# A hybrid attention and RWKV-7 layer on one core: the RWKV preparation laid out anew over the slots of the loop

## The chip, the cores and the metric

One core of a Trainium2 chip runs the whole program. The metric is device microseconds of one execution. The kernel before takes 1856.16 us (median of 3 runs, 1854.52 to 1862.93).

## The reference, cut to what matters

One layer over 1024 frames of width 1024: a projection, then attention with low-rank keys and values (8 heads) beside an RWKV-7 group (8 heads of 64), an output projection, cross-attention to 256 memory tokens, an MLP with squared ReLU, and norms between. The change lies in the RWKV group and its neighbours:

```
w_log = -softplus(-(w0 + tanh(w_l) @ w2)) - 0.5      # low-rank product "lw"
decay = exp(-exp(w_log))
a     = sigmoid(a0 + a_l @ a2)                        # low-rank product "la"
kk    = heads(k * k_k); kk /= max(norm(kk), 1e-12)    # sums of squares "ks"
k     = k * (1 + (a - 1) * k_a)
# per head and frame:
sa    = state @ (-kk_t)
state = state * decay_t + outer(sa, kk_t*a_t) + outer(v_t, k_t);  y_t = state @ r_t
y     = groupnorm(y) + sum(r * k * r_k) * v           # sums "rk", products "bv" (the bonus)
```

The recurrence is computed by chunks of 64 frames. Each chunk needs the inverse of a unit lower triangular 64x64 matrix built from products of keys ("al"). All is float32.

## The kernel before, in words

**Engines and order.** Each engine runs one list of instructions in the order in which it was written; waits are on counters (`Steps`) that name every step. Heads are taken in pairs, so the RWKV group has 4 pairs. Between 0 and about 390 us the core normalises, projects, and runs attention heads 0 to 5. Heads 6 and 7 follow, with the preparation of RWKV pair 0 beside them; then the RWKV loop over pairs 0 to 3, with the preparation of the next pair beside each (the memory tokens beside the last). From about 812 us on come the memory projections, the output projection, cross-attention and the MLP.

**The loop.** A pair has 8 windows of 128 frames, taken two at a time: 4 groups of 11 slots, 44 slots. In a group, TensorE does `double_q` and `double_z` twice (two levels that grow the inverse from blocks of 16 to 64; VectorE masks the first and adds the second), which are followed by slots 0, 1, 2, 3; then `solve`, `local`, `carry`, followed by slots 4, 5, 6; then four steps of `state`, `outputs`, and the next group's `scores` and `tokens`, followed by slots 7 to 10. VectorE's order around slots 4 to 6 is: slots 4 and 5, then the transition matrix (`mt`, line 2582: the carry product from PSUM plus a diagonal that GpSimd made), then slot 6, then per state one copy (line 2592) and for two of them the masked scores (line 2447). TensorE's first `state` of a group waits for `mt`.

**The preparation `prep(n, s)`** exists on TensorE, ScalarE, VectorE and GpSimd; slot s of one engine stands beside slot s of the others, and beside which work slot s comes is set by `beside` in the loop and by `beside_heads` in heads 6 and 7, which gives each of 18 places (9 a head) its slots. Its steps: TensorE lw0, lw1, la0, la1 (low-rank products, all in PSUM bank 7, so each waits for ScalarE's tanh of the one before), ks0, ks1 (sums of squares, each waits for a logarithm or square on ScalarE), al0 to al3 (16 products of 64x64 each, VectorE masks each), rk0, rk1 (bonus sums). VectorE kk, t1p, L (a scan), na, am, k2, nkk, kt, at, b, bt, rk, the masks of al, x0 and x1 (clearing the block table), bv0, bv1 and the substitution. ScalarE the tanh, square, logarithm and exponentials (W is the decay, Wi its inverse). GpSimd rt (needs W) and, after rk, kh and bh.

**The inverse.** The al matrices go from SBUF to DRAM in four stores (SyncE queue, `blocks`), come back as blocks of 16 by one load, and VectorE solves all blocks together: 15 steps j, each a product and a sum (`xm`, `xa`, lines 2412 and 2415), then a transposed copy (`xt`, 2418). Block and transpose are stored, and eight loads bring them back as chunks (`inverse`); the first doubling of a pair waits for four of them.

**Places.** `rAL` and `rXX` (al and inverse, two buffers each) lie in the attention's tiles: the outputs', queries', keys' and probabilities'. Pair 0's inverse lies over the probabilities. The last pair's slots hold the memory tokens' work: squares on ScalarE (slots 2, 3), sums on TensorE (slot 6), logarithm and exponential (slots 7, 8).

Of the kernel before, what the change touches and what calls it, by code (L numbers as in the profile page):

```python
# [12 lines left out]
ALU = mybir.AluOpType  # L13
# [14 lines left out]
SUBST = (range(0, 8), range(8, BLK - 1))  # L28
# [42 lines left out]
V_TILES = (0, 2, 3, 4, 7, 1, 5, 6)  # L71
# [93 lines left out]
def build(nc, x_t, mem_t, pos, wall, vecs, con_d, headw, wv_d, lora_d, out_t):  # L165
    with ExitStack() as ctx:
# [71 lines left out]
        def place(n):  # L238
# [232 lines left out]
        def each(names):  # L471
# [4 lines left out]
        P_ACT = Steps(sem("prep_act"), each(["tw0", "tw1", "ta0", "ta1", "kksq", "kl0", "kl1", "kf", "W", "Wi", "wt0", "wt1", "afirst"]))  # L476
        P_DVE = Steps(sem("prep_dve"), each(
            ["kk", "t1p", "L", "na", "am", "k2", "nkk", "kt", "at", "b", "bt", "rk",
             "al0", "al1", "al2", "al3", "x0", "x1", "bv0", "bv1"]
            + [x for j in range(BLK - 1) for x in (f"xm{j}", f"xa{j}")] + ["xt"]))  # L480
# [73 lines left out]
        def _(sp):  # L554
# [76 lines left out]
            def inverse(n):  # L631
# [9 lines left out]
                if n == 0:  # L641
                    sp.wait_ge(M_PE.sem, M_PE.at(f"o{MLA_HEADS - 1}_{NW - 1}", -1))
# [262 lines left out]
        def _(pe):  # L905
# [239 lines left out]
            def prep(n, s):  # L1145
# [14 lines left out]
                if s == 3:  # L1160
                    r_at(P_ACT, f"tw0_{n}")
                    low_rank(lora_wa[wa, 0:P], wa, T_CQWA, 7, 1).then_inc(sem_, one("lw1"))
                if s == 4:
                    r_at(P_ACT, f"tw1_{n}")
                    low_rank(lora_wa[wa, P:2 * P], wa, T_CQWA, 7, 0).then_inc(sem_, one("la0"))
                if s == 5:
                    r_at(P_ACT, f"ta0_{n}")
                    low_rank(lora_wa[wa, P:2 * P], wa, T_CQWA, 7, 1).then_inc(sem_, one("la1"))
# [214 lines left out]
            def beside(p, s):  # L1383
# [6 lines left out]
                elif s == 6:  # L1390
# [260 lines left out]
        def _(act):  # L1651
# [104 lines left out]
            def prep(n, s):  # L1756
# [5 lines left out]

                if s in (2, 3):
                    if s == 2 and n >= 1:
                        r_at(P_DVE, f"rk_{n - 1}")
                    r_at(P_PE, f"lw{s - 2}_{n}")
                    nc.scalar.activation(rT1[:, halves(s - 2)], PS[:, 7, :], ACT.Tanh, bias=vech[:, n:n + 1],
                                         scale=0.5).then_inc(sem_, one(f"tw{s - 2}"))
                if s in (4, 5):
                    r_at(P_PE, f"la{s - 4}_{n}")  # L1770
                    nc.scalar.activation(rA[:, halves(s - 4)], PS[:, 7, :], ACT.Tanh, bias=vech[:, 4 + n:5 + n],
                                         scale=0.5).then_inc(sem_, one(f"ta{s - 4}"))
# [10 lines left out]
                if s == 10:  # L1783
                    r_at(P_ACT, f"kl1_{n}")
                    nc.scalar.activation(rB[i], rB[i], ACT.Exp, scale=-0.5).then_inc(sem_, one("kf"))
# [4 lines left out]
                    nc.scalar.activation(rW, rWi, ACT.Exp, scale=-half_e).then_inc(sem_, one("W"))  # L1790
                if s == 11:
# [75 lines left out]
            def memory_step(s):  # L1867
# [3 lines left out]
                if s in (2, 3):  # L1871
                    act.wait_ge(mem_loaded, 32)
                    nc.scalar.activation(mem_sq[s - 2], mem_raw[s - 2], ACT.Square).then_inc(mm_act, 1)
                if s == 7:
# [3 lines left out]
                if s == 8:  # L1878
# [263 lines left out]
        def _(dve):  # L2142
# [182 lines left out]
            def prep(n, s):  # L2325
# [14 lines left out]
                if s == 4:  # L2340
                    r_at(P_ACT, f"tw1_{n}")
                    r(nc.vector.tensor_scalar(rT1, rT1, 1.0, None, ALU.add), "t1p")
                if s == 5:
# [4 lines left out]
                if s == 9:  # L2348
                    r_at(P_ACT, f"ta1_{n}")
                    r(nc.vector.tensor_scalar(rA, rA, -0.5, -0.5, ALU.mult, ALU.add), "na")  # L2350
                if s == 10:
                    own("na")
                    r(nc.vector.tensor_scalar(rT1, rA, 1.0, vec[:, V_KA + n:V_KA + n + 1], ALU.add, ALU.mult), "am")
                if s == 14:
# [19 lines left out]
                if s == 20:  # L2374
                    own("b")
                    r(nc.vector.tensor_tensor(rB[i], rA, rWi, ALU.mult), "bt")
                if s == 21:
                    r_at(P_POOL, f"rt_{n}")
                    r(nc.vector.scalar_tensor_tensor(r_, r_, vec[:, V_RK + n:V_RK + n + 1], rT1, ALU.mult, ALU.mult), "rk")
                if 22 <= s < 26:  # L2380
                    k = s - 22
# [9 lines left out]
                if s == 26:  # L2391
# [5 lines left out]
                if s in (26, 27):  # L2397
                    k = s - 26
# [4 lines left out]
                if 30 <= s < 37:  # L2403
                    for j in range(2 * (s - 30), 2 * (s - 30) + 2 + s // 36):
# [11 lines left out]
                if s == 36:  # L2416
# [562 lines left out]
```

## Time and profile before

| | |
|---|---|
| median of 3 runs | 1856.16 us |
| profiled execution, its own time | 1852.6 us |
| its span (first to last instruction) | 1850.5 us |
| TensorE busy | 1741.0 us, 94% |
| VectorE busy | 992.4 us, 54% |
| ScalarE busy | 793.5 us, 43% |
| GpSimd busy | 703.9 us, 38% |
| mean granted TensorE clock | 0.970 |

In rows, PE is TensorE (PEld its weight loads), DVE VectorE, ACT ScalarE, POOL GpSimd, SPq the SyncE queue; L12 is line 12 of the kernel; [...] is the idle time before an instruction and what ended it. A timeline row is start, duration (us), engine, line, operation, output<-input, count. A row of a window is its ends and length, then the busy time (and instructions) of PE, PEld, DVE, ACT and POOL, the granted clock, the share of the DMA engines and GB/s.

The granted clock is a share of 2.4 GHz: 1.00 is that level, 0.50 is 1.2 GHz. Matmuls are pipelined, so the durations of neighbours overlap. The chain that ended last is TensorE for 84% of the span and VectorE for 8%. Heads 6 and 7 take about 390 to 480 us, the four pairs of the loop about 484 to 812 us.

### The profile page before, as it was taken

To read this page: it belongs to the slowest core of one execution; us is meant where nothing else is said; L and a number is where in the kernel's file an instruction comes from. 1 tells how busy PE (TensorE), PEld (TensorE's weight loads), DVE (VectorE), ACT (ScalarE), POOL (GpSimd) and SP (SyncE) were. 2 spreads that over 40 slices of the span, in tenths; PEclk is the share of its full clock that TensorE was granted. 3 is DMA by queue.
4 is the path that set the end of the run, shared out by engine and by line. 5 is a ranking of instruction groups with operands and counts; after the bars stand their busy time and mean duration, and the time that the engine had idled before them with its cause. 6 is when DMAs were issued, how large, how long until landed. Compare 5 with 4: busy or idle time off the path is not lost.

```text
span 1850.5 us, 29970 instructions
## 1 busy us (share of the span) xinstructions
PE 1741.0 (94%) x11908; PEld 1332.4 (72%) x11908; DVE 992.4 (54%) x1549; ACT 793.5 (43%) x1530; POOL 703.9 (38%) x505
## 2 busy tenths in 40 slices
PE   4999999998788889899999999999999999999996
PEld 3766666655566666668898768778888888888885
DVE  6542232335464655463350262378856775884787
ACT  4313332244233343452130231367566666766762
POOL 1220211011120211232242202297695876968761
PEclk9999999988689999999999999999999999999998
DMA  5101010001111112242211101212112022020202
GB/s 195 53 24 32 23 34 10 21 5 29 41 19 42 20 43 42 88 145 87 88 41 51 34 1 34 76 50 69 50 42 92 23 69 67 26 92 23 69 1 91
DMA packets 81681, 94.35 MB, mean 51 GB/s; under 512 B 53648, under 2 KB 56208, under 8 KB 81552
## 3 DMA queue, kind: packets, MB, share of 16 engines
q1 hardware_dynamic: 81552, 92.56, 15.9%
q8 instruction: 89, 1.46, 0.3%
q14 instruction: 40, 0.33, 0.1%
HBM read 82.57 MB, written 9.98 MB: 50 GB/s over the span
## 4 chain that ended last, share of the span: by engine, by line
PE 84%; DVE 8%; issue 3%; ACT 2%; DMA 1%; POOL 1%; SPq 0%; DVEq 0%; ACTq 0%; POOLq 0%
PE PS L1615 32%; PE PS L922 16%; PE PS L970 8%; PE PS L1071 3%; PE PS L1106 2%; PE PS L1085 2%; PE PS L1140 2%; PE PS L1562 1%; PE PS L1541 1%; PE PS L1433 1%; PE PS L1143 1%; PE PS L1335 1%; PE PS L1418 1%; PE PS L1277 1%; PE PS L1030 1%
## 5 line engine op out<-in xcount | busy, mean ns | idle before, releaser
L1615 PE MATMUL PS<-memr,wsp 128*128 128x512 f32 x1332 | 321.2, 392 | 0.9 <-POOL wsp L883 0.9
L922 PE MATMUL PS<-xn,wsp 128*128 128x512 f32 x1344 | 309.6, 392 | 6.7 <-DVE xn L2158 6.7
L922 PEld LDWEIGHTS PS<-xn,wsp 128*128 128x128 f32 x1344 | 253.5, 189 | 62.0 <-DVE xn L2158 5.0
L1615 PEld LDWEIGHTS PS<-memr,wsp 128*128 128x128 f32 x1332 | 250.6, 188 | 56.0 <-POOL wsp L883 1.3
L762 POOL CAST wsp<-wraw 128x1024 fp32r<-128x1024 f32 x40 | 43.4, 1085 | 472.9 <-PE PS L922 306.5
L1615 PE MATMUL PS<-memr,wraw_r 128*128 128x512 f32 x684 | 167.7, 394 | 5.4 <-DVE memr L2721 3.3
L1615 PEld LDWEIGHTS PS<-memr,wraw_r 128*128 128x128 f32 x684 | 129.0, 189 | 35.2 <-DVE memr L2721 3.7
L970 PE MATMUL PS<-xn,wsp 128*128 128x512 f32 x576 | 146.7, 401 | 3.2 <-DVE proj L2208 3.1
L883 POOL TENSOR_TENSOR wsp<-sa,wsp 128x512 fp32r<-128x512 f32 x86 | 115.1, 1340 | 81.0 <-ACT wsp L2047 80.9
L970 PEld LDWEIGHTS PS<-xn,wsp 128*128 128x128 f32 x576 | 104.4, 188 | 40.1 <-issue 20.2
L2721 DVE TENSOR_TENSOR memr<-PS,memr 128x512 fp32r<-128x512 f32 x168 | 114.6, 682 | 27.4 <-ACT PS L2068 27.4
L1727 ACT ACTIVATE H<-PS,mst 128x128 f32<-128x128 f32 (+3 forms) x64 | 47.5, 741 | 179.8 <-DVE mst L2289 178.2
L1615 PE MATMUL PS<-tmp_r,wsp 128*128 128x512 f32 x444 | 116.9, 397 | 0.0
L2739 DVE TENSOR_TENSOR H<-PS,H 128x512 f32<-128x512 f32 x128 | 86.7, 688 | 46.7 <-PE PS L1615 30.1
L2289 DVE TENSOR_REDUCE mst<-PS 128x1 f32<-128x128 f32 (+3 forms) x64 | 48.2, 754 | 117.3 <-PE PS L1074 117.3
L2063 ACT CAST memr<-sa 128x512 fp32r<-128x512 f32 x96 | 59.2, 617 | 95.1 <-PE PS L1615 78.6
L1615 PEld LDWEIGHTS PS<-tmp_r,wsp 128*128 128x128 f32 x444 | 83.4, 188 | 21.2 <-DVE tmp_r L2721 1.3
L764 POOL TENSOR_TENSOR wsp<-wraw,wsp 128x1024 fp32r<-128x1024 f32 x40 | 96.4, 2410 | 3.2
L867 POOL TENSOR_TENSOR sbx<-sa,sbx 128x512 f32<-128x512 f32 x64 | 85.9, 1342 | 4.7
L883 POOL TENSOR_TENSOR wsp<-sbx,wsp 128x512 fp32r<-128x512 f32 x62 | 82.9, 1341 | 11.1 <-ACT wsp L2047 11.0
L847 POOL TENSOR_TENSOR ssum<-con,rsm 64x256 f32<-64x256 f32 x32 | 27.3, 871 | 139.5 <-DVE ssum L2582 139.5
L1071 PE MATMUL PS<-H 128*128 128x512 f32 (+2 forms) x192 | 77.2, 512 | 0.0
(336 smaller groups left out, 3157.4 us busy)
## 6 DMA issues: line engine op xcount, KB each, us to landing
wraw<-in_weights_dram SPq DMA_DIRECT2D x40, 512.0 KB, 3.6
sa<-in_weights_dram SPq DMA_DIRECT2D x32, 512.0 KB, 4.3
H<-in_x_dram SPq DMA_DIRECT2D x16, 512.0 KB, 6.5
sbx<-in_weights_dram SPq DMA_DIRECT2D x32, 256.0 KB, 2.6
sa<-in_weights_dram SPq DMA_DIRECT2D x32, 256.0 KB, 2.6
H<-in_weights_dram SPq DMA_DIRECT2D x8, 512.0 KB, 6.7
out_dram<-sbx SPq DMA_DIRECT2D x16, 256.0 KB, 2.1
a_dram<-H SPq DMA_DIRECT2D x16, 128.0 KB, 2.5
```

Source lines behind the costliest of these rows:

```text
L764: nc.gpsimd.tensor_tensor(wsp[:, k, :, 1, :], raw, wsp[:, k, :, 0, :].bitcast(F32), ALU.subtract).then_inc(w_split, 1)
L867: nc.gpsimd.tensor_tensor(out, a, b, op).then_inc(W_SUM.sem, W_SUM.one(name))
L883: nc.gpsimd.tensor_tensor(w[:, 1, :], w_source(g), w[:, 0, :].bitcast(F32), ALU.subtract).then_inc(mw_rest, 1)
L922: last = nc.tensor.matmul(PS[:, 2 * k + half, :], wsp[:, k, kt, a, :], src[:, at, b, HALF * half:HALF * half + HALF], start=(i == 0 and (a ...
L970: last = nc.tensor.matmul(PS[:, bank, :], wsp[:, u % 2, kt, a, :], xn[:, kt, b, HALF * half:HALF * half + HALF], start=(kt == 0 and (a, b) ...
L1071: nc.tensor.matmul(PS[:, b + part, 0:n], mQ[:, win(q)], mK[:, HALF * part:HALF * part + n], start=True, stop=(part < q // 4))
L1615: last = nc.tensor.matmul(PS[:, g % PS_BANKS, :], w[:, a, win(k)], x[:, b, :], start=(k == 0 and (a, b) == (0, 0)), stop=(k == ROWS - 1 an ...
L1727: nc.scalar.activation(mP[q % 2][:, 0:n], two(2 * (q % 2))[:, 0:n], ACT.Exp, bias=mNeg[hd][:, q:q + 1], accum_out=mSum[h // 2 % 2][:, c:c ...
L2063: nc.scalar.copy(x_split_of(d)[:, 0, :], x_source(d)).then_inc(mx_head, 1)
L2289: m(nc.vector.tensor_reduce(mNeg[h % 2][:, q:q + 1], two(2 * (q % 2))[:, 0:P * (q + 1)], AX_X, ALU.max, negate=True), f"m{h}_{q}")
L2721: nc.vector.tensor_tensor(x[:, 1, :], PS[:, PS_BANKS + d % 2, :], x[:, 0, :].bitcast(F32), ALU.subtract).then_inc(mx_rest, 1)
L2739: out(nc.vector.tensor_tensor(tile, a, b, ALU.add), f"{kind}{part}_{v}")
```

## The change

Slots are laid out anew, and places with them; no instruction is added or taken away.

- TensorE and ScalarE: the four low-rank products and their tanh go from slots 2 to 5 to slots 0 to 3; al0 to al3 from 22-25 to 18-21; rk0 and rk1 from 26, 27 to 31, 32.
- VectorE: t1p and L to slot 3 (beside kk), na and am to 4, k2 from 14 to 5, bt from 20 to 16, the masks of al to 18-21 and rk behind them in 21, x0 and x1 from 26 to 24, bv0 and bv1 to 31 and 32.
- Substitution: steps 0 to 14 in slots 30 to 36 before; after, 0-3 in 26, 4-7 in 27, 8 in 29, 9 in 30, 10 and 11 in 31, 12 and 13 in 32, 14 (and the transposed copy) in 33.
- ScalarE in slot 10: W ahead of kf.
- Places: the first inverse (`rXX[0]`) lies over queries and keys, `rAL[1]` over probabilities; the loads of the first inverse wait for the last scores instead of the last attention values. `V_TILES`, the order in which tiles of H take memory weights and x, follows.
- Last pair: squares in slots 5 and 6, sums in slot 9, logarithm and exponential in 10 and 11.

```diff
-SUBST = (range(0, 8), range(8, BLK - 1))
+SUBST = {26: (0, 1, 2, 3), 27: (4, 5, 6, 7), 29: (8,), 30: (9,), 31: (10, 11), 32: (12, 13), 33: (14,)}
+BONUS = 31
-V_TILES = (0, 2, 3, 4, 7, 1, 5, 6)
+V_TILES = (0, 1, 2, 4, 7, 3, 5, 6)
...
-        rAL = [hs_[:, S * n:S * n + S].rearrange("p (w h n) -> p w h n", w=NW, h=2) for n in range(2)]
-        rXX = [hs_[:, 3072 + 2048 * n:5120 + 2048 * n].rearrange("p (a w h n) -> p a w h n", a=2, w=NW, h=2)
-               for n in range(2)]
+        rAL = [hs_[:, t:t + S].rearrange("p (w h n) -> p w h n", w=NW, h=2) for t in (0, 3072)]
+        rXX = [hs_[:, t:t + 2048].rearrange("p (a w h n) -> p a w h n", a=2, w=NW, h=2) for t in (1024, 5120)]
...
             i = 9 * (h - BESIDE) + q
-            if i < 8:
-                return (2 * i + 1, 2 * i + 2) if h >= BESIDE else ()
-            return ((17, 20), (21,), (22, 23), (24, 25), (26, 27), (), (30, 31), (32, 33), (34, 35), (36,))[i - 8]
+            if h < BESIDE:
+                return ()
+            if i < 9:
+                return (2 * i, 2 * i + 1)
+            return ((), (18, 19), (20, 21, 22), (24,), (), (26, 27), (29, 30, 31), (32, 33), ())[i - 9]
...
                 if n == 0:
-                    sp.wait_ge(M_PE.sem, M_PE.at(f"o{MLA_HEADS - 1}_{NW - 1}", -1))
+                    sp.wait_ge(M_PE.sem, M_PE.at(f"s{MLA_HEADS - 1}_{NW - 1}", -1))
...                                                                         # TensorE
-                if s == 2:
+                if s == 0:
                     pe.wait_ge(lora_loaded, 16 * (n + 1))
...                                                                         # lw1, la0, la1: slots 1, 2, 3
-                if 22 <= s < 26:
-                    k = s - 22
+                if 18 <= s < 22:
+                    k = s - 18
                     if k == 0:
                         r_at(P_ACT, f"kl1_{n}")
-                        r_at(P_DVE, f"rk_{n}")
+                        r_at(P_DVE, f"bt_{n}")
...
-                if s == 26:
-                    r_at(P_DVE, f"al3_{n}")
+                if s == BONUS:
+                    r_at(P_DVE, f"rk_{n}")
                     block_sums(0, C_BO, proj[:, T_R + n, :], 7).then_inc(sem_, one("rk0"))
-                if s == 27:
+                if s == BONUS + 1:
...                                                                         # ScalarE
                 if s == 10:
-                    r_at(P_ACT, f"kl1_{n}")
-                    nc.scalar.activation(rB[i], rB[i], ACT.Exp, scale=-0.5).then_inc(sem_, one("kf"))
                     r_at(P_DVE, f"L_{n}")
...
                     nc.scalar.activation(rW, rWi, ACT.Exp, scale=-half_e).then_inc(sem_, one("W"))
+                    r_at(P_ACT, f"kl1_{n}")
+                    nc.scalar.activation(rB[i], rB[i], ACT.Exp, scale=-0.5).then_inc(sem_, one("kf"))
...
-                if s in (2, 3):
+                if s in (5, 6):
                     act.wait_ge(mem_loaded, 32)
...                                                                         # VectorE: the slots listed above
-                if 30 <= s < 37:
-                    for j in range(2 * (s - 30), 2 * (s - 30) + 2 + s // 36):
+                if s in SUBST:
+                    for j in SUBST[s]:
```

## Rows read from the trace of the kernel before

**Rows 1.** page, busy time of TensorE: us, share, instructions.
```profile
PE 1741.0 (94%) x11908; PEld 1332.4 (72%) x11908; DVE 992.4 (54%) x1549; ACT 793.5 (43%) x1530; POOL 703.9 (38%) x505
```

**Rows 2.** PE's waits, 480 to 812 us (total us, times, longest).
```profile
PE PS L1366 <- DVE ssum L2582: 11.1, 6, 3.1
```

**Rows 3.** timeline of pair 1, group 1 (start, us, engine, line).
```profile
603.11 2.35 POOL L792 TENSOR_TENSOR sa<-proj,sa 128x1024 f32<-128x1024 f32 x1 [30.47 <-ACT sa L1790]
...
604.06 2.48 DVE L2356 SCALAR_TENSOR_TENSOR sa<-sa,proj 128x1024 f32<-128x1024 f32 x1
...
611.82 0.68 DVE L2582 TENSOR_TENSOR ssum<-PS,ssum 128x512 f32<-128x512 f32 x1
...
612.55 0.45 PE L1366 MATMUL PS<-tmp,ssum 128*64 128x64 f32 x4 [3.10 <-DVE ssum L2582]
```

**Rows 4.** windows: doubling in groups 0 to 3, then three state chains.
```profile
578.20:584.11 5.91, 5.44 (x84) 3.31 (x84) 3.14 (x9) 0.69 (x1) 0.00 (x0) 1.00 0.58 159
600.05:603.83 3.78, 3.50 (x87) 2.78 (x83) 2.25 (x7) 3.77 (x6) 0.72 (x1) 1.00 0.02 4
619.70:624.38 4.68, 4.61 (x153) 4.37 (x151) 3.46 (x11) 1.22 (x2) 3.51 (x2) 1.00 0.11 25
639.88:644.93 5.05, 3.24 (x86) 2.69 (x83) 4.30 (x21) 2.34 (x4) 0.00 (x0) 1.00 0.00 0
612.55:619.70 7.15, 6.50 (x87) 5.13 (x88) 4.48 (x8) 2.08 (x9) 1.49 (x3) 0.76 0.01 2
632.67:639.88 7.21, 6.30 (x94) 4.43 (x94) 4.23 (x18) 3.54 (x11) 1.07 (x2) 1.00 0.01 2
653.55:659.50 5.95, 5.04 (x87) 3.90 (x88) 2.38 (x6) 2.02 (x9) 1.07 (x2) 1.00 0.74 168
```

**Rows 5.** groups of VectorE instructions by line: busy us, mean ns of one.
```profile
L2415 DVE TENSOR_TENSOR sc_s<-sc_s 128x15 f32<-128x15 f32 (+7 forms) x60 | 12.5, 208 | 2.1
...
L2347 DVE TENSOR_TENSOR_SCAN sa<-step,sa 128x1024 f32<-128x1024 f32 x4 | 9.2, 2289 | 0.1
...
L2402 DVE TENSOR_TENSOR proj<-PS,proj 128x512 f32<-128x512 f32 x8 | 5.5, 692 | 14.8 <-PE PS L1143 14.7
...
L2353 DVE TENSOR_SCALAR sa<-sa,vec 128x1024 f32<-128x1024 f32 x4 | 3.0, 740 | 0.0
```

**Rows 6.** timeline of head 6: the same k2 with GpSimd idle.
```profile
423.49 1.21 DVE L2356 SCALAR_TENSOR_TENSOR sa<-sa,proj 128x1024 f32<-128x1024 f32 x1
```

**Rows 7.** timeline, then DMA issues (last: us to landing), pair 1.
```profile
624.58 0.42 DVE L2387 TENSOR_TENSOR H<-PS,con 128x256 f32<-128x256 f32 x1 [0.39 <-PE PS L1187]
...
628.17 0.37 SPq L629 DMA_DIRECT2D sc_s<-a_dram  x1
...
sc_s<-a_dram SPq DMA_DIRECT2D x1, 128.0 KB, 3.2
```

**Rows 8.** stretches at the lower clock: busy by engine, granted clock.
```profile
477.80:511.40 33.60, 29.41 (x268) 20.62 (x266) 8.35 (x19) 8.23 (x18) 4.37 (x3) 0.50 0.20 49
532.40:540.00 7.60, 6.93 (x74) 5.48 (x76) 4.63 (x10) 1.27 (x6) 1.18 (x2) 0.56 0.01 2
...
644.90:648.30 3.40, 3.37 (x44) 3.15 (x44) 3.16 (x10) 0.74 (x2) 0.00 (x0) 0.50 0.23 28
...
750.80:754.00 3.20, 3.20 (x67) 2.85 (x65) 0.00 (x0) 1.66 (x2) 0.00 (x0) 0.50 0.36 141
```

**Rows 9.** timeline of the last pair, group 0.
```profile
746.25 1.06 ACT L1873 ACTIVATE sa<-sa 128x1024 f32<-128x1024 f32 x1 [2.44 <-DMA sa<-in_mem_dram]
...
748.56 0.34 PE L1323 MATMUL PS<-sc_w,sc_s 64*64 64x64 f32 x8 [2.23 <-ACT sc_s L1951]
```

**Rows 10.** timeline of head 7: bonus sum, transposes of block 6.
```profile
453.05 1.13 PE L1143 MATMUL PS<-proj,con 128*128 128x512 f32 x2 [1.63 <-DVE proj L2402]
...
466.61 0.96 PE L1085 MATMUL PS<-con,H 128*128 128x128 f32 x7 [1.68 <-ACT H L1736]
```

**Rows 11.** chain of waits ahead of the loop: start, us, what.
```profile
474.87 4.07 DMA xt_dram<-sc_s
```

More of the change, by code:

```diff
@@ L475, in build @@
                                            "rk0", "rk1"]))
-        P_ACT = Steps(sem("prep_act"), each(["tw0", "tw1", "ta0", "ta1", "kksq", "kl0", "kl1", "kf", "W", "Wi", "wt0", "wt1", "afirst"]))
+        P_ACT = Steps(sem("prep_act"), each(["tw0", "tw1", "ta0", "ta1", "kksq", "kl0", "kl1", "W", "kf", "Wi", "wt0", "wt1", "afirst"]))
         P_DVE = Steps(sem("prep_dve"), each(
-            ["kk", "t1p", "L", "na", "am", "k2", "nkk", "kt", "at", "b", "bt", "rk",
-             "al0", "al1", "al2", "al3", "x0", "x1", "bv0", "bv1"]
-            + [x for j in range(BLK - 1) for x in (f"xm{j}", f"xa{j}")] + ["xt"]))
+            ["kk", "t1p", "L", "na", "am", "k2", "nkk", "kt", "at", "b", "bt", "al0", "al1", "al2", "al3", "rk", "x0", "x1"]
+            + [x for place in SUBST for x in ([f"bv{place - BONUS}"] if place in (BONUS, BONUS + 1) else [])
+               + [y for j in SUBST[place] for y in (f"xm{j}", f"xa{j}")]] + ["xt"]))
         P_POOL = Steps(sem("prep_pool"), each(["rt", "kh", "bh"]))
@@ L1159, in prep @@
                     low_rank(lora_wa[wa, 0:P], wa, T_CQWA, 7, 0).then_inc(sem_, one("lw0"))
-                if s == 3:
+                if s == 1:
                     r_at(P_ACT, f"tw0_{n}")
                     low_rank(lora_wa[wa, 0:P], wa, T_CQWA, 7, 1).then_inc(sem_, one("lw1"))
-                if s == 4:
+                if s == 2:
                     r_at(P_ACT, f"tw1_{n}")
                     low_rank(lora_wa[wa, P:2 * P], wa, T_CQWA, 7, 0).then_inc(sem_, one("la0"))
-                if s == 5:
+                if s == 3:
                     r_at(P_ACT, f"ta0_{n}")
@@ L1389, in beside @@
                     prep(p + 1, s)
-                elif s == 6:
+                elif s == 9:
                     memory_sums()
@@ L1761, in one @@
                     return P_ACT.one(f"{name}_{n}")
-                if s in (2, 3):
[L1764 to L1772, printed above, removed]
+                if s in (0, 1):
+                    if s == 0 and n >= 1:
+                        r_at(P_DVE, f"rk_{n - 1}")
+                    r_at(P_PE, f"lw{s}_{n}")
+                    nc.scalar.activation(rT1[:, halves(s)], PS[:, 7, :], ACT.Tanh, bias=vech[:, n:n + 1],
+                                         scale=0.5).then_inc(sem_, one(f"tw{s}"))
+                if s in (2, 3):
+                    r_at(P_PE, f"la{s - 2}_{n}")
+                    nc.scalar.activation(rA[:, halves(s - 2)], PS[:, 7, :], ACT.Tanh, bias=vech[:, 4 + n:5 + n],
+                                         scale=0.5).then_inc(sem_, one(f"ta{s - 2}"))
                 if s == 5:
@@ L1877, in memory_step @@
                                          scale=1.0 / D).then_inc(mm_act, 1)
-                if s == 8:
+                if s == 11:
                     act.wait_ge(mm_act, 3)
@@ L2347, in prep @@
                     r(nc.vector.tensor_tensor_scan(rWi, rStep, rT1, 0.0, ALU.mult, ALU.add), "L")
-                if s == 9:
+                if s == 4:
                     r_at(P_ACT, f"ta1_{n}")
                     r(nc.vector.tensor_scalar(rA, rA, -0.5, -0.5, ALU.mult, ALU.add), "na")
-                if s == 10:
+                if s == 4:
                     own("na")
                     r(nc.vector.tensor_scalar(rT1, rA, 1.0, vec[:, V_KA + n:V_KA + n + 1], ALU.add, ALU.mult), "am")
-                if s == 14:
+                if s == 5:
                     own("am")
@@ L2373, in prep @@
                     r(nc.vector.tensor_tensor(rA, rA, rKK, ALU.mult), "b")
-                if s == 20:
+                if s == 16:
                     own("b")
                     r(nc.vector.tensor_tensor(rB[i], rA, rWi, ALU.mult), "bt")
[L2377 to L2381, printed above, removed]
+                if 18 <= s < 22:
+                    k = s - 18
                     r_at(P_PE, f"al{k}_{n}")
@@ L2390, in prep @@
                         f"al{k}")
-                if s == 26:
+                if s == 21:
+                    r_at(P_POOL, f"rt_{n}")
+                    r(nc.vector.scalar_tensor_tensor(r_, r_, vec[:, V_RK + n:V_RK + n + 1], rT1, ALU.mult, ALU.mult), "rk")
+                if s == 24:
                     if n >= 1:
@@ L2396, in prep @@
                     r(nc.vector.memset(sc_s[:, 3456:3712:BLK + 1], 1.0), "x1")
-                if s in (26, 27):
-                    k = s - 26
+                if s in (BONUS, BONUS + 1):
+                    k = s - BONUS
                     r_at(P_PE, f"rk{k}_{n}")
```

10 lines of the change are left out of this document (5 added, 5 removed).

## The prediction

> **What bounds the kernel.** I read the page first, then the rows of who waited for whom on TensorE, then the timeline of one pair of the RWKV loop, then busy time and granted clock by stretch, and last the chain of waits ahead of the loop. TensorE (PE) is busy 94% of the span [rows 1], and everything outside 390 to 812 us is untouched but for places of buffers. So the question is what PE loses inside that stretch. It holds heads 6 and 7 of the attention (to about 480 us, with the first pair's preparation beside them) and four pairs of about 82 us, each of four groups. A group is: doubling (a ping-pong of small products and VectorE masks, slots 0 to 3), solve, local and carry (slots 4 to 6), then the chain of four states (slots 7 to 10). The next pair's preparation is cut into 44 slots over these groups, in program order on every engine, so a long VectorE step in a slot holds whatever the loop wants of VectorE behind it.
>
> The largest such loss is PE waiting for the transition matrix (the sum that reads the carry product): 11.1 us in 6 waits [rows 2]. The timeline of group 1 shows why: VectorE begins five preparation steps at 604.06 (k2, nkk, kt, at, b), reaches the matrix at 611.82, and PE starts again at 612.55, 3.1 us late [rows 3]. Three pairs have this wait. The rest is spread: doubling in group 3, where substitution sits in slots 0 to 3, takes 5.05 us against 3.78 in a group with nothing beside it [rows 4], and waits are followed by stretches at the lower clock level.
>
> **The change, part by part.** Terms are per pair unless said; gains are negative.
>
> *Low-rank products two slots sooner (pairs 1 and 2, group 0).* Doubling with two of them takes 5.91 us, without any 3.78 [rows 4]: 1.06 each, none of it hidden. Two move from the solve part into doubling: the same PE time. VectorE then has all of kk, t1p, the scan, na, am and k2 before the matrix: 2.29 for the scan [rows 5], four simple ones of at most 0.74 [rows 5], k2 at 1.21 as it runs when GpSimd leaves it alone [rows 6]: 6.4 us. PE needs 5.6 us from the end of doubling (603.83 [rows 4]) to its wait (612.55 less 3.10 [rows 3]) and has a key sum of 1.06 in slot 6 to fill the rest. So the matrix is just about not late, and the wait that the key sum had for the squared keys goes. I take -0.5, between +1.0 (it is late and nothing fills) and -1.0.
>
> *k2 out of group 1, bt into it, W ahead of kf.* Five steps before, five after: k2 (2.48 us [rows 3]) gives way to bt, which has the shape of k2 alone (1.21). k2 was long because it started while GpSimd's rt ran (603.11 for 2.35) [rows 3]: 605.46 plus 1.2 is its end. With W first, rt starts some 1.05 us sooner and overlaps the first step by some 0.35 instead of 1.27. So 7.76 becomes 6.85: -0.9, and a wait of 2.2 remains. Bounds: -2.1 if rt is out of the way wholly, 0 if nkk inherits the whole delay. The Trainium skill, "SBUF — State Buffer", section "Who interferes with whom", says that an instruction of VectorE with two inputs in SBUF and one of GpSimd that reads SBUF exclude each other, whoever came first, with no sharing. By that rule moving bt in front of the matrix costs its full turn behind any diagonal product, and the term would be nearer 0; the row on k2 agrees with it.
>
> *Score products of the inverse (al) from slots 22-25 to 18-21.* Beside doubling the four cost 4.68 less 3.78, 0.9 in all [rows 4]: -0.9 there. In the state chain of group 1 they come instead of bt and rk alone. That chain takes 7.15 us (at a mean clock of 0.76), a bare one 5.95 [rows 4]. I take +1.2, between 0 (the chain's own gaps take them) and +3.5 (they are paid in full at the lower level).
>
> *Substitution and bonus sums in group 2.* The two bonus sums have the shape of a low-rank product: -2.1 from the solve part. There VectorE now does 16 substitution instructions of 0.21 [rows 5], with their gaps 0.235: 3.75 us inside PE's 5.6. But they need the blocks read back. Before, the last mask begins at 624.58, the read is issued at 628.17 and lands 3.2 us later [rows 7]: 6.8 from mask to landing. The mask will lie about 0.8 ahead of doubling, VectorE is free for slot 4 some 4.0 after doubling begins (604.06 less 600.05 [rows 3, 4]), so it waits about 2.0 and ends 5.7 after that point: 0.1 to 0.2 over. Net -1.9. In the state chain of group 2 (7.21 with one sum of the post step and 12 substitution instructions [rows 4]) come two bonus sums, 2.1, and their two VectorE products of 0.69 [rows 5], one of them in front of a state copy: +2.6, between +1.5 and +4.
>
> *Group 3's doubling freed.* 5.05 becomes 3.8 to 3.9 (the last step and the transpose stay in slot 0): -1.2. The stretch at half clock right behind it, 644.9 to 648.3 with PE busy 3.37 of 3.40 [rows 8], and its like one pair later (two in all) should not arise: -1.7 each. The inverse ends three slots sooner, in front of loads that are hidden in most pairs: nothing counted.
>
> *Last pair.* ScalarE squares the memory tokens in slots 2 and 3, waits there for the load, and so copies the solved product late: PE idles 2.23 us [rows 9] and 3.2 us at half clock follow with PE busy throughout [rows 8]: 1.6. Behind both copies, in slots 5 and 6, the load (there at 746.25 [rows 9]) has landed: -3.5 with a little left. The memory sums move into the state chain at the same PE cost: 0.
>
> *Heads 6 and 7.* The second bonus sum no longer waits 1.63 for the first [rows 10], and both sums (2.1) go where PE waits for row maxima (1.68 at 466.61 [rows 10]); against that, eight more substitution instructions sit before the maximum of block 6 (+2.0, partly the same wait), and in head 6 lw1 waits for its tanh (0.8) while the key sums, now in one place, wait for one logarithm (1.7) instead of one square (1.7). I get -1.6 at the loop's start; bounds +3 and -5. The first pair's inverse may now be loaded once the last scores have read queries and keys. Its loads waited for the transpose's store (474.87 plus 4.07 [rows 11]), not for the attention's end, so this alone is 0; what counts is that the substitution ends about 2.3 sooner, which is in the -1.6.
>
> *First group of the loop.* 477.8 to 511.4 is at 1.2 GHz, PE busy 29.4 of 33.6 [rows 8]. Full clock would give back up to half of that. With four dense low-rank products inside doubling instead of two the rise may come sooner; the trace can't say. I take -2 of bounds +2 and -8.
>
> **Sum.** Group 0 twice -0.5: -1.0. Three times (-0.9 +1.2 -0.9 -1.9 +2.6 -1.2): -3.3. Clock behind group 3: -3.4. Last pair -3.5. Heads -1.6. First group -2.0. Together -14.8. The profiled execution took 1852.6 us (span 1850.5), so 1837.8; the median of the runs shown is 3.6 above it, so 1841.4. What lies behind the loop is PE-bound and moves with it.
>
> **Rivals.**
> A, the loss moves instead of going (28%). The state chain is serial between PE and VectorE; if al masks, bonus products and sums are paid in full there (+3.5 and +4 for +1.2 and +2.6: 11.1 more in three pairs), only -3.7 is left: 1852. For it: four states in 5.95 us leave 1.5 a step, and a sum of 1.06 with a product of 0.69 does not fit beside one. Against: the 12 substitution instructions and one sum added only 1.26 to it [rows 4].
> B, slower (12%): the block read is late. VectorE waits for it in slot 4 of group 2 in front of the matrix, PE idles behind. Up to about 6.8 us from mask to landing it costs nothing; each us more is one us in three pairs, and the idle of 3.1 us in group 1 was followed by up to 7.6 us at half clock (3.8 lost) [rows 8]. With store and read stretched from 3.6 and 3.2 to 5.7 each, 4.6 too late: 3 x (4.6 + 3.8) = 25 over the forecast, 1866.6. The threshold is the place where the sum has no slack at all; against it, the landing is the same transfer in the same company as before.
> C, the clock (inside my 60%): if the first group rises early and group 1 no longer drops, another 10 off: 1831.
>
> **How the numbers follow.** Forecast 60% (C in its lower part), A 28%, B 12%. A change of 0.5% (9.3 us) is about what a measurement of this kernel tells from none, so faster means below 1846.9 and slower above 1865.4. Nearly all of the forecast case is faster with a little of A; the forecast's upper tail joins A in same; B splits: faster 0.60, same 0.33, slower 0.07. Range 1831 to 1857: it holds the forecast case and A, and leaves out most of B and the far end of C.
>
> **What would show it.** Right: PE's wait for the matrix in group 1 is near 2.2, none over 1 in group 0; doubling of group 2 and 3 near 3.8; the state chain of group 2 near 9.8; no wait for a square in the last pair; substitution 0 to 7 starts about 2 us after VectorE is free. Wrong: group 2's matrix late by more than 1 us, new half-clock stretches behind the longer chains, or heads 6 and 7 longer than before.

## The result, and the profile after

| | before | after |
|---|---|---|
| median (runs) | 1856.16 us (11) | 1839.88 us (11) |
| profiled span | 1850.5 us | 1835.3 us |
| start of the loop | 484.13 us | 479.03 us |
| first `state` of the loop's last group | 808.66 us | 792.01 us |

The ratio is 0.9904, 95% interval 0.9887 to 0.9921. The forecast was 1841.4. The same kernel run once more, in a later series (x_again below), gave 1837.54 (6 runs).

Three names are used for the parts of a group: *doubling* runs from the first `double_q` product to the first `solve` product, the *solve part* from there to the first `state`, the *chain* from the first `state` to the next group's doubling.

First the busy times of the page. TensorE's hardly moved against [rows 1]: work was not taken away, waiting was.

```profile
PE 1737.6 (95%) x11908; PEld 1332.5 (73%) x11908; DVE 991.6 (54%) x1549; ACT 791.8 (43%) x1528; POOL 705.0 (38%) x505
```

PE's wait for the matrix over the whole span (total us, times, longest) is 9.2 us, to be laid beside [rows 2]; the longest is 2.3 instead of 3.1.

```profile
PE PS L1368 <- DVE ssum L2584: 9.2, 7, 2.3
```

The timeline of pair 1, group 1, to be laid beside [rows 3]. GpSimd's rt now starts 1.9 us ahead of VectorE's first step (nkk), not 0.95; nkk, kt and at take 1.55 to 1.63 beside GpSimd's instructions (at took 1.19 before, with GpSimd idle), b and bt 1.2. The five steps last 6.96 us up to the matrix instead of 7.76, and PE starts its first `state` 2.29 us late.

```profile
592.47 2.37 POOL L794 TENSOR_TENSOR sa<-proj,sa 128x1024 f32<-128x1024 f32 x1 [27.94 <-ACT sa L1790]
594.80 3.14 POOL L849 TENSOR_TENSOR ssum<-con,rsm 64x256 f32<-64x256 f32 x2
...
594.36 1.55 DVE L2361 SCALAR_TENSOR_TENSOR sa<-sa 128x1024 f32<-128x1024 f32 x1
595.84 1.63 DVE L2365 TENSOR_TENSOR proj<-sa 128x1024 f32<-128x1024 f32 x1
597.39 1.61 DVE L2370 TENSOR_TENSOR sa<-sa 128x1008 f32<-128x1008 f32 x1
598.93 1.21 DVE L2375 TENSOR_TENSOR sa<-sa 128x1024 f32<-128x1024 f32 x1
600.17 1.22 DVE L2378 TENSOR_TENSOR sa<-sa 128x1024 f32<-128x1024 f32 x1
601.32 0.68 DVE L2584 TENSOR_TENSOR ssum<-PS,ssum 128x512 f32<-128x512 f32 x1
...
602.06 0.45 PE L1368 MATMUL PS<-tmp,ssum 128*64 128x64 f32 x4 [2.29 <-DVE ssum L2584]
```

Windows after: a stretch at the lower clock behind that wait; the chain of group 2 of pair 1; and the chain of group 1 of pair 2. They answer to the chains of [rows 4] and the stretches of [rows 8]. Behind the same wait the clock fell in pairs 0 and 1 (about 14 us each, 525 to 539 and 603.5 to 617.5) and not in pair 2; before, it fell behind group 1 in all three pairs, for some 7, 4 and 7 us. Of the stretches behind group 3 (644.9 to 648.3 before, and its like) none is left.

```profile
603.00:618.00 15.00, 14.65 (x212) 12.88 (x206) 6.98 (x19) 3.44 (x11) 4.08 (x3) 0.54 0.21 41
...
624.71:632.53 7.82, 7.60 (x97) 4.64 (x97) 4.63 (x16) 3.71 (x11) 0.91 (x2) 1.00 0.01 2
683.10:690.06 6.96, 6.96 (x151) 6.15 (x152) 3.51 (x11) 2.15 (x9) 1.18 (x2) 1.00 0.20 44
```

**Where the 15.2 us of the span came from**, from the starts of the groups in the two timelines, beside the terms of the forecast:

| stretch | forecast | measured |
|---|---|---|
| up to the start of the loop (heads 6 and 7) | -1.6 | -5.1 (-1.05 of it ahead of head 6, in code that is the same) |
| pair 0, group 0 | -2.0 | -3.8 |
| group 0 of pairs 1 and 2 | -1.0 | -1.3 |
| group 1 of three pairs | +0.9 | +2.1 |
| group 2 of three pairs | -0.6 | -1.1 |
| group 3 of three pairs, with the clock behind it | -7.0 | -5.5 |
| last pair, up to the first `state` of its last group | -3.5 | -2.0 |
| behind that | 0 | +1.5 |
| together | -14.8 | -15.2 |

The +1.5 behind the loop goes with an early start: that part takes 1043.2 to 1043.3 us in the three kernels whose loop starts at 478 to 479 us (after, x_again, x_bonus) and 1040.2 to 1042.2 in all others.

### The profile page after: what moved, and what is told of

It reads as the page before. It is cut to its first block, busy times and chain, and to the rows that moved or that the text cites. A ratio compares the mean times of both kernels' runs of the same rounds, so it can differ in the third digit from the quotient of the medians.

```text
span 1835.3 us, 29968 instructions
## 1 busy us (share of the span) xinstructions
PE 1737.6 (95%) x11908; PEld 1332.5 (73%) x11908; DVE 991.6 (54%) x1549; ACT 791.8 (43%) x1528; POOL 705.0 (38%) x505
## 4 chain that ended last, share of the span: by engine, by line
PE 85%; DVE 8%; issue 2%; ACT 2%; POOL 1%; DMA 1%; SPq 0%; DVEq 0%; ACTq 0%; POOLq 0%
PE PS L1617 32%; PE PS L924 16%; PE PS L972 8%; PE PS L1073 3%; PE PS L1108 2%; PE PS L1087 2%; PE PS L1142 2%; PE PS L1564 2%; PE PS L1543 1%; PE PS L1435 1%; PE PS L1337 1%; PE PS L1420 1%; PE PS L1145 1%; PE PS L1032 1%; PE PS L1279 1%
## 5 line engine op out<-in xcount | busy, mean ns | idle before, releaser
L885 POOL TENSOR_TENSOR wsp<-sbx,wsp 128x512 fp32r<-128x512 f32 x62 | 83.1, 1344 | 10.9 <-ACT wsp L2049 10.8
```

What stands on the lines that cost most here:

```text
L885: nc.gpsimd.tensor_tensor(w[:, 1, :], w_source(g), w[:, 0, :].bitcast(F32), ALU.subtract).then_inc(mw_rest, 1)
```

## Experiments

All were timed against the kernel before, whose median was 1856.8 to 1861.4 in those series; ratios are to that median. "Loop" is the time from the first doubling of pair 0 to the first `state` of the last group: 324.5 us before, 313.0 after. "Starts" is when it begins: 484.1 and 479.0. Times of parts are from the profiled execution. In the edits ... marks lines that are left out.

**x_mem: the kernel before with only the memory tokens' work moved.**

```
-                elif s == 6:                    +                elif s == 9:
-                if s in (2, 3):  # squares      +                if s in (5, 6):
...                                                              # logarithm, exponential: slots 10, 11
```

> The kernel before with one edit: the memory tokens' squares in slots 5 and 6 of the last pair instead of 2 and 3, their sums in 9, logarithm and exponential in 10 and 11. Theory S (the gain is the sum of the slots' terms): the last pair's group 0 loses its 2.2 us wait and the stretch at half clock behind it, -2.8 to -3.5 us, about 1853. Rival (the load is late wherever it is waited for, or the memory sums stretch the state chain by as much): no difference, 1856.

1852.69 us (12 runs), ratio 0.9978 (0.9959 to 0.9998). Group 0 of the last pair takes 19.44 us instead of 22.47, at full clock throughout:

```profile
744.61:764.05 19.44, 17.72 (x320) 14.28 (x318) 7.56 (x17) 7.81 (x18) 4.51 (x4) 1.00 0.53 194
```

So 3 us of the forecast's 3.5 are there, by themselves. Here and in the whole change 0.8 of it is paid back in the next group (17.02 and 17.01 instead of 16.20).

**x_lr: the kernel before with only the low-rank products two slots sooner**, and what follows from them on VectorE up to k2, with W ahead of kf. Substitution, bt, al, bonus and memory stay.

> The kernel before with the low-rank products in slots 0 to 3, t1p and the scan in 3, na and am in 4, k2 in 5, and W ahead of kf; bt, al, bonus sums and substitution where they were. Theory S: group 1 has four VectorE steps before the matrix, its wait falls from 3.1 to about 1.0 us, group 0 changes by less than 1: -6 us by waits alone, down to -10 if the half-clock stretches behind group 1 go too: 1846 to 1850. Rival (the wait moves to group 0, where VectorE has 6.4 us before the matrix): at least 1 us of wait there in each pair and no more than -3 in all, 1853 or more.

1848.95 us (12 runs), ratio 0.9941 (0.9917 to 0.9965). The loop takes 314.6 us though the last pair's group 0 grew to 27.13 (ScalarE reaches the squares sooner, waits 5.20 us for the load, and holds the copies of the solved product; PE idles 4.98 us, and some 10 us at the lower clock follow). The wait of group 1 is 1.03 us, shorter than in the kernel after:

```profile
612.43 0.45 PE L1368 MATMUL PS<-tmp,ssum 128*64 128x64 f32 x4 [1.03 <-DVE ssum L2584]
```

Group 1 takes 16.45 us in pairs 0 and 1 (20.45 and 19.65 before), and in pair 2 17.64. The kernel after then puts bt (1.22 us) into this place: 1.03 plus 1.22 is 2.25 of its 2.29. The loop starts 7.6 us later than in the kernel before, which took most of the gain.

Here bt and rk are in the chain of group 1, as before, and where the clock stays up it takes 6.01 us, next to a bare one's 5.95 [rows 4]. In pair 2 the clock fell for 4 us behind the same wait of 1.03, and the chain takes 7.20.

```profile
612.43:618.44 6.01, 5.16 (x86) 4.02 (x88) 4.31 (x8) 2.03 (x9) 1.48 (x3) 1.00 0.01 3
```

Pairs 0 to 2 together take 242.7 us of this loop and 247.7 of the kernel after's. So in these profiles the steps that the kernel after moves besides (bt, al, bonus sums, substitution) cost more than they brought, as long as the wait of 2.29 us stays in; x_bonus and x_subst below show that the last two pay, which leaves bt and al. An estimate for this kernel with x_mem's edit, from the last pair's group 0 at 19.44 us instead of 27.13 and 0.8 paid back in the next: a loop of some 308 us, 5 below the kernel after. It was not run.

**x_late: the kernel after with the blocks read twice**, the second read in front of the substitution: rival B made true.

```
-                sp.dma_start(bA, blocks_in_dram(0)).then_inc(a_blocks_loaded, 16)
+                for k in range(2):
+                    sp.dma_start(bA, blocks_in_dram(0)).then_inc(a_blocks_loaded, 16)
+                    sp.wait_ge(a_blocks_loaded, 16 * (2 * n + k + 1))
...                                                              # VectorE waits for 32 * (n + 1)
```

> The kernel after, with the blocks of the inverse read twice in a row, so that substitution's input is there about 3.7 us later. Theory S with the mechanism of rival B: the matrix of group 2 comes 3 to 4 us later in each of three pairs, and half-clock stretches may follow: 1850 to 1860, against 1840 for the kernel after. Other theory (substitution has slack, since pairs 0 and 1 run at half clock there): at most +4, 1844 or less.

1851.22 us (12 runs), ratio 0.9965 (0.9943 to 0.9988): 11.3 above the kernel after, and the loop 12.9 longer. In pair 1 VectorE waits 5.62 us for the blocks and PE 3.56 for the matrix (2.29 in pair 0, 2.72 in pair 2), with 3.5 to 7 us at half clock behind each:

```profile
631.30 0.69 PE L1370 MATMUL PS<-tmp,ssum 128*64 128x64 f32 x4 [3.56 <-DVE ssum L2586]
...
631.30:641.45 10.15, 10.15 (x92) 6.05 (x94) 4.63 (x16) 3.18 (x10) 1.18 (x2) 0.70 0.01 2
```

The mechanism of B is real. In the kernel after the read lands in time: the same wait of VectorE is 1.13 us in pair 1 and 1.87 in pair 2, and PE reaches its first `state` after 6.50 us in both. In pair 1 VectorE still waits 0.38 us for the carry product before the matrix; in pair 2 the matrix stands directly behind the substitution, so there the slack is used up and nothing is lost.

**x_fill: the kernel after with PE kept busy in the wait of group 1.** Four 128x512 products whose result nothing reads go into slot 17. VectorE's work, and the time of the matrix, stay as they are.

```
+                if s == 17 and n >= 1:
+                    r_at(P_ACT, f"kl1_{n}")
+                    for _ in range(2):
+                        block_sums(0, C_BO, proj[:, T_GK, :], 7)
```

> The kernel after, with four extra matmuls of 128x512 (2.1 us, result unused) in slot 17 of pairs 0 to 2, where PE otherwise waits 2.29 us for the matrix of group 1. Theory I (it is this idle time that the clock answers to): no half-clock stretch begins behind group 1 in pairs 0 and 1, and their state chains fall from 10.2 to about 7 us, doubling of group 2 from 5.9 to 4.7: -8 to -9 us, about 1832. Theory W (it is the many small products around it, or chance of phase): the stretches stay and the time is 1840 or up to 1 us more.

1831.25 us (5 runs), ratio 0.9854 (0.9822 to 0.9887). Doubling, solve and matrix take what they took (solve to first state 7.92), but the idle is 0.38 instead of 2.29, and the chain behind is 6.97 in all three pairs:

```profile
602.21 1.98 PE L1145 MATMUL PS<-proj,con 128*128 128x512 f32 x4
...
604.83 0.45 PE L1372 MATMUL PS<-tmp,ssum 128*64 128x64 f32 x4 [0.38 <-DVE ssum L2588]
...
604.83:611.80 6.97, 6.97 (x151) 6.16 (x153) 3.51 (x11) 2.16 (x9) 1.18 (x2) 1.00 0.19 41
```

Adding work took 8.6 us off the median (6.3 against the later median of the kernel after), and 8.3 off the loop. VectorE's list up to the matrix is as long as it was, and the matrix comes at the same point, so it is PE's idle that costs: the chain that took 10.2 us in pairs 0 and 1 is the same instructions at the lower clock.

**x_warm: x_fill with 20 more such products around the first pair's scores**, to raise the clock for group 0 of pair 0.

```
...                                                              # warm(count): count pairs of 128x512 products
+                warm({scores: 2, tokens: 0, a_v: 8}[stage])
```

> The kernel with fillers in group 1's wait (1831), and ten extra matmul pairs of 128x512 around the first pair's scores: 2 pairs behind the scores, 8 behind the products a_v, where PE otherwise waits about 3 us for the inverse; results unused. Theory I: the clock is back at 2.4 GHz before or soon after the first doubling, and the first group takes 21 to 26 us instead of 33: less some 4 us of extra work, -3 to -8, 1823 to 1828. Rival (the half-clock stretch lasts as long whatever PE does): +6 to +14, since the fillers run at half clock and end behind the arrival of the inverse.

1831.69 us (5 runs), ratio 0.9855 (0.9835 to 0.9875). Group 0 of pair 0 falls from 33.3 us in x_fill to 27.44, and the loop starts at 489.82 instead of 485.66. The clock is up for the first 7 us of the loop and then half for 7 us (496.5 to 503.5), where x_fill has it at half for 21 us. The expectation, 21 to 26 us for the group and 1823 to 1828, was missed: the fillers cost what they bring in the median.

**x_bonus: the kernel after with the bonus sums back in slots 26 and 27** (`BONUS = 26`).

> The kernel after with the two bonus sums and their products back in slots 26 and 27 (solve part of group 2). By the prediction's terms (-2.1 from the solve part, +2.6 in the chain) this move lost 0.5 per pair, so undoing it gives -1.5: 1838. By the trace of the kernel after, where the chain of group 2 is 7.85 us and not 9.8, the sums cost the chain only 0.8, and undoing the move costs 1 to 1.3 per pair: +3 to +4, about 1843.

1848.91 us (11 runs), ratio 0.9958 (0.9943 to 0.9973). In pair 1 solve to first state is 9.58 us instead of 6.50, the chain 6.78 instead of 7.82:

```profile
618.23:627.81 9.58, 8.68 (x139) 5.49 (x139) 5.23 (x20) 3.46 (x6) 0.00 (x0) 1.00 0.14 23
```

The pair of sums (2.1 us) costs 1.04 in the chain and 3.08 in the solve part, where VectorE's products of them also stand in front of the substitution and PE waits 0.90 us for the matrix. Doubling of group 3 takes 3.83 us here and 4.33 in the kernel after, whose second bonus product stands in slot 32, right ahead of the first mask. So a pair pays 1.5 us for the sums in their new place and 3.1 in the old. The loop takes 319.9 us, 6.9 more than after; the median rose by 9.0, not by the 3 to 4 expected. Per pair the parts give 1.5; the rest of the loop's loss is the clock, which fell behind group 1 in pair 2 as well (22.48 instead of 18.67 us).

**x_subst: the kernel after with the substitution back in slots 30 to 36.**

> The kernel after with the substitution back in slots 30 to 36. Theory S: doubling of group 3 goes from 4.3 back to 5.1 or more and its half-clock stretch returns, the state chain of group 2 gains a little, and in head 7 the substitution ends later, which delays the first pair: +4 to +9, 1844 to 1849. Rival (the gain came from the other parts): within 2 us of 1840.

1849.41 us (12 runs), ratio 0.9963 (0.9943 to 0.9982). The solve part of group 2 takes 5.45 us to the matrix without substitution and 5.46 with eight steps; the chain takes 7.82 either way (six steps in both). Doubling of group 3 is 5.65 instead of 4.34:

```profile
637.51:643.16 5.65, 3.24 (x87) 2.70 (x83) 5.24 (x26) 2.12 (x4) 0.00 (x0) 1.00 0.00 0
```

The loop is 318.3 us and starts at 487.23. The stretch at half clock behind group 3 came back in pair 1 (643 to 647 us), not in pair 2. So substitution costs nothing in the solve part, where VectorE has time to spare, and next to nothing in the chain; beside doubling, where each mask holds PE, it costs 1.3 us.

**x_kf: the kernel after with kf ahead of W again**, one term by itself.

> The kernel after with the exponentials kf and W in their order of before. The prediction gave W's earlier place (and k2's going) 0.9 us: PE's wait for the matrix of group 1 should be about 3.1 instead of 2.29 in three pairs, and the time 2 to 3 us above the kernel after (1842). Rival: the wait is set by VectorE's own work and not by GpSimd's product, then 2.3 stays and the time is the same.

1846.18 us (6 runs), ratio 0.9945 (0.9925 to 0.9964). The wait is 3.22 to 3.23 us in all three pairs, which is the predicted 0.9. The first step beside GpSimd's rt takes 2.49 us, here nkk, as k2 took 2.48 before [rows 3]: the delay belongs to the place and not to the step. The median rose by 6 to 9, not by 2 to 3: behind the longer wait the clock fell in pair 2 as well, so that group 1 takes 23.2 to 23.5 us everywhere (21.9, 21.9 and 18.7 in the kernel after).

```profile
600.60 2.49 DVE L2361 SCALAR_TENSOR_TENSOR sa<-sa 128x1024 f32<-128x1024 f32 x1
...
609.23 0.45 PE L1368 MATMUL PS<-tmp,ssum 128*64 128x64 f32 x4 [3.22 <-DVE ssum L2584]
...
690.72:701.25 10.53, 10.53 (x147) 9.36 (x149) 3.66 (x10) 1.95 (x8) 1.18 (x2) 0.56 0.13 29
```

**x_nkk: the kernel after with kf in slot 8 of ScalarE and nkk in slot 9 of VectorE**, in the gaps of group 0's chain.

```
+                if s == 8:
+                    r_at(P_ACT, f"kl1_{n}")
+                    nc.scalar.activation(rB[i], rB[i], ACT.Exp, scale=-0.5).then_inc(sem_, one("kf"))
...                                                              # kf leaves slot 10
-                if s == 14:   # nkk             +                if s == 9:
```

> The kernel after with kf in ScalarE's slot 8 and nkk in VectorE's slot 9 (state chain of group 0) instead of 14. Theory S: one step of 1.13 us less before the matrix of group 1, its wait falls from 2.29 to about 1.1, the chain of group 0 grows by at most 0.5: -2 to -3 by waits. Theory I (the clock answers to the idle time): with 1.1 us of wait no half-clock stretch begins there, another -4.5 in each pair that had one: 1829 to 1838. If the clock answers to something else, 1837.

1829.77 us (5 runs), ratio 0.9847 (0.9831 to 0.9862): the lowest median, 10.1 under the kernel after (7.8 under its later one), though not apart from x_fill, x_warm and x_best by its interval. Nkk takes 1.23 us where it is now, the chain of group 0 grows by 0.13, VectorE itself waits 0.45 for the carry product, and group 1 takes 16.94 us in all three pairs:

```profile
590.62 1.23 DVE L2362 SCALAR_TENSOR_TENSOR sa<-sa 128x1024 f32<-128x1024 f32 x1 [1.36 <-ACT sa L1787]
...
602.28 0.45 PE L1368 MATMUL PS<-tmp,ssum 128*64 128x64 f32 x4 [0.59 <-DVE ssum L2585]
```

Its loop is 299.5 us, 13.5 less than after; it starts 7.7 later.

**x_best: x_nkk with step 14 and the transposed copy in slot 32.**

> The kernel after with kf in slot 8 and nkk in slot 9 (as in the run that took the wait of group 1 away), and with step 14 and the transposed copy in slot 32 instead of 33. If slot 32 hides them, doubling of group 3 falls from 4.33 to 3.8 us and the chain of group 2 stays at 7.8: 1.6 us under that run, 1828 us. If one of the two products (0.21) and the copy delays a state copy of the chain, the chain grows by what doubling loses and the time is the same, 1830.

1831.06 us (4 runs), ratio 0.9850 (0.9828 to 0.9872). A miss: doubling of group 3 rose from 4.33 to 5.14 in pairs 0 to 2. Slot 32 is the last of the chain, and what VectorE does there stands ahead of the first mask, like rk below; in slot 33 it stands behind it.

**x_rk: x_nkk with rk in slot 25** instead of 21, and steps 6 and 7 moved from slot 27 into the chain.

> The kernel with kf in slot 8 and nkk in slot 9, and besides the product rk taken from slot 21 (1.27 us on VectorE, ahead of the first mask of group 2's doubling) to slot 25, and four steps of the substitution in slots 26 and 27 taken apart: 4 and 5 stay in slot 27, 6 and 7 in 29, 8 and 9 in 30. If rk is what holds doubling of group 2 at 4.66 us, that falls to about 3.8 in three pairs, the substitution waits less for its blocks, the matrix is not late and the chain of group 2 stays at 7.8: 2.6 us less, about 1827. If the block read sets the matrix, doubling falls and the part from solve to the matrix grows from 5.45 by as much: 1830. If the chain pays for four more products and sums of 0.22 each, it grows to about 8.7 and the time is 1830 too.

1835.22 us (4 runs), ratio 0.9857 (0.9812 to 0.9902). Doubling of group 2 fell to 4.00 us (from 4.66), but PE waited 1.6 us for the matrix (2.9 in pair 0, with the lower clock behind it), by none of the ways I had listed. The loop takes 306.0 us, 6.5 more than in x_nkk; by the ratios alone the two are not apart. GpSimd's kh and bh wait for rk; they now run beside the first substitution steps, a product of 15 elements a partition takes 0.72 us and the sum behind it, 0.18 otherwise, takes 1.86:

```profile
689.51 1.93 POOL L799 TENSOR_TENSOR sa<-proj,sa 128x1024 f32<-128x1024 f32 x1 [11.13 <-DVE proj L2399]
691.40 1.93 POOL L803 TENSOR_TENSOR sa<-sa 128x1024 f32<-128x1024 f32 x1
...
690.76 0.72 DVE L2415 TENSOR_TENSOR sc_s<-sc_s 128x15 f32<-128x15 f32 x1 [1.33 <-DMA sc_s<-a_dram]
691.52 1.86 DVE L2418 TENSOR_TENSOR sc_s<-sc_s 128x15 f32<-128x15 f32 x1
...
696.45 0.45 PE L1368 MATMUL PS<-tmp,ssum 128*64 128x64 f32 x4 [1.64 <-DVE ssum L2585]
```

The Trainium skill, "SBUF — State Buffer", section "Who interferes with whom", says that a VectorE instruction with two inputs in SBUF and a GpSimd instruction that reads SBUF exclude each other for the whole instruction. This trace agrees: the sum starts 0.12 us behind the second GpSimd product, which takes 1.93, and ends 0.05 us behind it.

**x_again: the kernel after, once more.**

> The kernel after, unchanged. Four kernels with the same code in heads 6 and 7 began the loop between 478.9 and 485.7 us. If that is a difference between executions, this one may begin it anywhere there, with a half-clock stretch near 445 us in the later case, and the loop from there to the last state takes 313 us as before. If it belongs to the kernels, it begins at 479.

1837.54 us (6 runs), ratio 0.9906 (0.9889 to 0.9923). The loop takes 313.0 us again and starts at 478.19; the clock falls behind the wait in pairs 0 and 1 and not in 2, as in the first profile of this kernel. Of the four kernels that the expectation counts as having the same code in heads 6 and 7, only the kernel after and x_fill have it: x_late reads the blocks twice there, and x_bonus has its sums elsewhere.

## Why the prediction was right, point by point

Most mechanisms were right, but the total is nearer than its parts: several errors cancelled, which is luck. The loop was forecast at -13.2 us and came at -11.5; the rest is heads 6 and 7, whose -5.1 isn't settled. In group 2 the terms of doubling and chain were wrong by 5.9 and 5.5 us over the three pairs, in opposite directions. And one sign of being wrong, new half-clock stretches behind a longer chain, did come, behind group 1.

- **Group 0, -0.5 a pair.** -0.67 and -0.62. Doubling grew by 1.64, the solve part to the first state shrank by 2.31, and no wait for the matrix came. Right. The four low-rank products cost doubling less than the 1.06 each that was priced in (7.55 us with four, 5.91 with two). x_lr shows that this edit, with W ahead of kf, is what makes most of the loop's gain possible.
- **Wait of group 1, 3.1 to 2.2.** 2.29; x_kf gives 0.93 to the order of W and kf alone. Right, also in that a part of nkk's delay stayed (1.55). GpSimd's two diagonal products now lie beside kt and at, which gave back 0.4 on at; bt ran behind them at 1.22, so the reading by which it would wait its full turn, and the term be nearer 0, did not come true.
- **Al in that chain, +1.2.** A mis-sized term. At full clock the chain takes 6.01 us with bt and rk (x_lr) and 6.96 with al, so the work itself costs 0.95. The 7.15 us that I set it on top of had a stretch at the lower clock in it already (mean clock 0.76). So pair 2, whose clock stayed up, gained 0.8 (7.78 to 6.96), while the chains of pairs 0 and 1 at the lower level take 10.2, +2.3 and +3.1, and pull 1.3 more into doubling of group 2 (5.92 instead of 4.66). Group 1 as a whole was forecast at +0.9 and came at +2.1. The stretch behind the wait was 4 to 7 us long before and 14 after where it came; x_fill and x_nkk show that it hangs on the idle ahead of it. What sets its length stays open: behind the same wait and in the same chain it is 3.5 us in pair 1 of x_late and 17 in pair 1 of x_bonus.
- **Doubling of group 2, -0.9.** Wrong: +0.2 at full clock (4.45 to 4.66), and +1.5 in pairs 0 and 1. (Rows 4 end this doubling at 624.38; its first `solve` product starts at 624.15, which makes it 4.45 and al's share 0.67.) The al products left it, but I passed over rk, which now stands behind the last al mask and so ahead of the first doubling mask: 1.27 us of VectorE in front of PE. X_rk takes it away and doubling falls by 0.66.
- **Solve part of group 2, -1.9.** -2.2 in all three pairs, without a wait for the blocks that PE sees. Right.
- **Chain of group 2, +2.6 (9.8 us).** Mis-sized: +0.77 (7.05 to 7.82). I had added the bonus sums in full, but the chain had gaps for half of them or more (1.04 of 2.1 us in x_bonus), and two more steps of substitution cost it 0.05 (7.82 us with six, 7.87 with eight in x_rk). Rival A rested on this full price; x_bonus shows the chain to be the cheap place. This error and the one on doubling offset each other.
- **Group 3.** Doubling 4.34 (forecast 3.8 to 3.9): -0.7 a pair, not -1.2. What is left is the second bonus product in slot 32: without it doubling takes 3.83 (x_bonus). The clock behind it: gone as forecast in pairs 1 and 2, but at 1.2 each (solve part 8.79 to 7.55) and not 1.7. Another 0.9 came from pair 0, where PE had waited 0.75 us for the inverse's load ahead of the next pair and no longer does; the prediction counted nothing for that, so its -3.4 is met by luck.
- **Last pair, -3.5.** Group 0 -2.8, and +0.8 in group 1. A little over half of it remained; the mechanism is right (x_mem), the price in group 1 was left out.
- **First group, -2.** -3.8, inside its bounds.
- **Heads, -1.6.** -5.1 in the profile, but this term isn't settled. X_fill has the same instructions in heads 6 and 7 as the kernel after and starts the loop at 485.66, with a stretch at the lower clock at 444 to 455 that the kernel after does not have; x_again (478.19) and x_bonus (478.92) do not have it either, x_subst and x_nkk do. Whether the place of the code in the program or something between executions decides stays open; the two profiles of the kernel after (479.03 and 478.19) speak for the first, but one repeat does not settle it. The heads of the kernel before scatter too: x_mem has the same and starts at 486.10, not 484.13. The loop, 11.5 us shorter in both profiles of the kernel after, is the part of the gain that is shown.
- **Rival C** (inside the forecast) came true in part: the clock rose at about 498 us instead of 512 in the first group, but stayed up behind group 1 only in pair 2. With that wait removed it stays up in all three, and x_fill and x_nkk come at 1831 and 1830.

## What to carry to other kernels

Read a list of moved steps for what each engine does just ahead of an instruction that another engine waits for: rk before a mask, bt before the matrix and step 14 before a mask were small steps in dear places, while rk and bt in a chain with gaps cost next to nothing (6.01 us against 5.95). A short idle of TensorE can cost more behind it than in itself, so price the wait and the stretch that follows together, and try filling it before shortening the other engine's list. When a step moves, move its dependents in your head as well: x_rk lost its gain to two GpSimd products that only waited for it. And measure the groups of a change apart before you keep all of it: here the first edit alone (x_lr) had a shorter loop in pairs 0 to 2 than the whole.

## What the runs showed of the hardware

- **Idle and clock.** Group 1 of pairs 0 to 2, wait of PE, and time of the chain behind it, which is 6.96 us at full clock with al in it:

| kernels | wait | chain |
|---|---|---|
| x_fill, x_warm | 0.37 | 6.96 in 6 of 6 |
| x_nkk, x_best, x_rk | 0.59 | 6.96 in 9 of 9 |
| after, x_again, x_late, x_bonus, x_subst | 2.3 | 8.5 to 11.5 in 12 of 15, 6.96 in 3 |
| x_kf | 3.2 | 10.5 to 10.8 in 3 of 3 |
| x_lr (bt and rk in the chain, 6.01 at full clock) | 1.03 | 7.20 in 1 of 3, 6.01 in 2 |
| before, x_mem (the same chain) | 3.1 | 7.15 to 8.19 in 6 of 6 |

 The length of the wait alone does not decide: 2.3 us was followed by the lower clock in 12 of 15 cases, 1.03 in one of three, and waits of 1.6 us in group 2 of x_rk in neither of two. In those stretches PE shows as busy (14.65 of 15.00 us in the window above) and VectorE at less than half (6.98 us); only the granted clock tells the loss.
- **VectorE beside GpSimd.** A VectorE sum that started right behind a GpSimd product ended with it: 0.18 us became 1.86 beside one of 1.93. A step of 1.23 us took 1.55 where it overlapped the end of GpSimd's rt by 0.48 (after), and 2.49 where it overlapped rt by 1.4 (x_kf).
